# A hybrid decoder layer on one core: branch B's softmax exchange carried unit by unit and back in halves, with five smaller changes of order

## What is computed

```python
h = x @ w_in                                   # q, k, v, gate of both branches, two merge gates
# branch A: 16 heads of 64, 2 key/value heads, rope, causal window of 128, a sink logit per head
o_a = banded_attention(rope(qa), rope(ka), va, 127, sink=sinks)
# branch B: 4 heads of 128 in each of 3 groups, windows 128, 512, 2048 at dilations 1, 4, 16
for gi, (window, dilation) in enumerate(((128, 1), (512, 4), (2048, 16))):
    outs[gi], lses[gi] = dilated_group(rope(qb)[gi], rope(kb)[gi], vb[gi], window, dilation)
o_b = sum(softmax(lses, axis=0)[..., None] * outs)      # one softmax over the three groups
y_a = (o_a * silu(gate_a)) @ w_pa
y_b = (o_b * silu(gate_b)) @ w_pb
merged = sigmoid(mg_a + b0) * y_a + sigmoid(mg_b + b1) * y_b
out = layer_norm(1.189 * x + merged @ w_out, ln_g, ln_b)
```

## Time and profile before

| What | Value |
|---|---|
| Runs (three) | 1388.90, 1389.39, 1390.16 us, median 1389.39 |
| The profiled execution, device time | 1388.75 us |
| Span of its instructions | 1387.0 us |
| PE busy (matmuls) | 1360.5 us, 98% |
| PE busy in the last stretch, 1330 to 1387 | 43.6 of 57 us |
| ACT, POOL, DVE busy | 574.5, 669.8, 477.4 us (41, 48, 34%) |
| Granted TensorE clock, mean | 0.997 of full speed |

### The profile page before, as it was taken

How to read it: one execution, slowest core, us unless ns; L and a number is a source line. 1 busy time by engine, 2 the same in 40 slices (tenths; PEclk the granted TensorE clock), 3 DMA queues, 4 the chain that set the end, 5 groups by cost and what they waited for, 6 DMA issues and landing times.

```text
span 1387.0 us, 19876 instructions
## 1 busy us (share of the span) xinstructions
PE 1360.5 (98%) x6488; PEld 1154.3 (83%) x6488; DVE 477.4 (34%) x846; ACT 574.5 (41%) x971; POOL 669.8 (48%) x512
## 2 busy tenths in 40 slices
PE   9999999999999999999999999999999999999996
PEld 7888888778988988898898888888888888888884
DVE  5866565652031223203111011010101202287688
ACT  5455464543472365347237322222222222445442
POOL 4633443454555545455454465464555636422214
PEclk9999999999999999999999999999999999999998
DMA  8432241435374354337434343653536446377664
GB/s 260 131 122 76 76 136 52 130 111 119 93 168 137 87 120 135 119 92 163 147 110 137 88 149 113 151 129 102 177 91 157 122 130 147 95 248 259 208 241 152
DMA packets 204990, 190.07 MB, mean 137 GB/s; under 512 B 16528, under 2 KB 178576, under 8 KB 204944
## 3 DMA queue, kind: packets, MB, share of 16 engines
q1 hardware_dynamic: 191344, 151.74, 37.1%
q0 software_dynamic: 13600, 37.75, 11.0%
HBM read 185.23 MB, written 41.94 MB: 164 GB/s over the span
## 4 chain that ended last, share of the span: by engine, by line
PE 50%; issue 25%; POOL 20%; DVE 2%; ACT 1%; DMA 1%; POOLq 0%; SPq 0%; DVEq 0%; ACTq 0%
PE acc L1493 45%; POOL w_lo L574 11%; POOL w_lo L573 9%; PE ps_scores L1493 2%; PE ps_out L1493 1%; PE ps_turn L1493 1%; PE ps_out L1582 0%; DMA raw<-xT 0%; DMA raw<-w_in 0%; DVE w_lo L1290 0%; POOL q_left L599 0%; POOL q_left L601 0%; DVE x_lo L981 0%; DVE z L1351 0%; ACT both_stats L655 0%
## 5 line engine op out<-in xcount | busy, mean ns | idle before, releaser
L573 POOL TENSOR_TENSOR w_lo<-raw,w_hi 128x512 fp32r<-128x512 f32 x241 | 319.3, 1325 | 700.8 <-ACT w_hi L627 577.3
L1493 PE MATMUL acc<-x_hi,w_hi 128*128 128x512 f32 x1216 | 478.2, 393 | 5.8 <-POOL w_lo L574 3.2
L1493 PE MATMUL acc<-x_hi,w_lo 128*128 128x512 f32 x1216 | 474.2, 390 | 0.0
L1493 PE MATMUL acc<-x_lo,w_hi 128*128 128x512 f32 x1216 | 474.1, 390 | 0.0
L627 ACT ACTIVATE w_hi<-raw 128x1024 fp32r<-128x1024 f32 x224 | 234.5, 1056 | 337.2 <-PE acc L1493 332.5
L574 POOL TENSOR_TENSOR w_lo<-raw,w_hi 128x512 fp32r<-128x512 f32 x241 | 332.4, 1379 | 0.0
L1493 PEld LDWEIGHTS acc<-x_hi,w_hi 128*128 128x128 f32 x1216 | 228.5, 188 | 51.2 <-POOL w_lo L574 3.9
L1493 PEld LDWEIGHTS acc<-x_hi,w_lo 128*128 128x128 f32 x1216 | 228.2, 188 | 48.3
L1493 PEld LDWEIGHTS acc<-x_lo,w_hi 128*128 128x128 f32 x1216 | 228.5, 188 | 44.1
L1216 DVE TENSOR_TENSOR part_a<-acc,part_a 128x512 f32<-128x512 f32 x16 | 11.1, 691 | 321.7 <-PE acc L1493 321.7
L1493 PE MATMUL acc<-w_hi,x_lo 128*128 128x384 f32 x256 | 85.6, 334 | 0.0
(11 more groups left out here) (265 smaller groups left out, 1621.3 us busy)
## 6 DMA issues: line engine op xcount, KB each, us to landing
raw<-w_in SPq DMA_DIRECT2D x384, 128.0 KB, 2.3
q_left<-w_out POOLq DMA_DIRECT2D x12, 2048.0 KB, 13.6
raw<-w_in SPq DMA_DIRECT2D x256, 96.0 KB, 2.5
raw<-q_left SPq DMA_DIRECT2D x32, 512.0 KB, 4.8
raw<-w_in SPq DMA_DIRECT2D x64, 192.0 KB, 2.9
raw<-w_pa SPq DMA_DIRECT2D x64, 128.0 KB, 6.2
raw<-w_out SPq DMA_DIRECT2D x16, 512.0 KB, 4.2
raw<-xT SPq DMA_DIRECT2D x8, 512.0 KB, 4.7
```

What stands on the lines that cost most here:

```text
L573: nc.gpsimd.tensor_tensor(dst[:, left], raw[:, slot, left], hi[:, left].bitcast(F32), ALU.subtract)
L1493: ins = nc.tensor.matmul(into[:, 0:cols], s, m, start=start and k == 0, stop=stop and k == n - 1)
```

## The change

The change has six parts. No work is added or left out; two line numbers that the text names for the changed kernel are its own.

1. **The first job.** The matmuls of job 0 are reordered: all four high-by-high ones first (they wait for `w_hi` and `x_hi` only), then four of `w_lo` by `x_hi` after the low part of the weights, then four of `w_hi` by `x_lo` after the first `x_lo`.
2. **Branch A's values.** The low part of the probabilities comes last (order hi-hi, v_lo by probsT_hi, v_hi by probsT_lo, each over both key blocks), and the wait for it (`probsT_rest`) is moved from before the first matmul to before the third kind. This touches 32 units.
3. **Ropes.** `rope` is split in a cosine and a sine part, and the bank is given back by the cosine product. In the first head's group 0, the cosine product of tile 2 is put ahead of tile 1's sine product and sum.
4. **The exchange.** `collect` is done unit by unit, 4 copies a unit, one unit at a time from block 3 on (in the merge from block 1 on); `spread` in two halves of 8 copies, at its block and one later, with the divisions of units 2 and 3 waiting for one half each. The numbers of both plans change.
5. **The last stage, who makes what.** The low part of job 53 goes from DVE to POOL and that of job 54 from POOL to DVE.
6. **The last stage, when.** `row_root(1)` on ACT moves from job 49 to job 50 in its list, `row_far(1, 3)` on DVE from job 51 to job 54.

The diff, cut to its core:

```diff
-def head_stages(scores, apart, collect, mix, weigh, factor, spread, division, turn, values, gate):
+def head_stages(scores, apart, collect, mix, weigh, factor, spread, division, turn, values, gate, together=1):
...
+    for u in range(B_UNITS):
+        plan.setdefault(collect + u * apart, []).append(("collect", u))
+    for name, start in (("mix", mix), ("weigh", weigh), ("factor", factor), ("spread", spread), ("gate", gate)):
         plan.setdefault(start, []).append((name, 0))
+    plan.setdefault(spread + together, []).append(("spread", 1))
...
-B_PLAN = head_stages(1, 2, 9, 11, 12, 13, 14, 17, 19, 21, 28)
-B_PLAN_MERGE = head_stages(0, 1, 4, 5, 5, 6, 6, 7, 8, 9, 13)
+B_PLAN = head_stages(1, 2, 3, 10, 11, 12, 14, 16, 18, 20, 28)
+B_PLAN_MERGE = head_stages(0, 1, 1, 5, 5, 6, 7, 7, 8, 9, 13)
...
-POOL_LOW = (0, 1, 16, 17, 18, 32, 33, 34, 35, 44, 46, 50, 52, 54)
+POOL_LOW = (0, 1, 16, 17, 18, 32, 33, 34, 35, 44, 46, 50, 52, 53)
...
-            def collect(i, first_unit):
+            def collect(b, i, first_unit):
-                act.wait_ge(probs_ready, first_unit + B_UNITS)
+                act.wait_ge(probs_ready, first_unit + b + 1)
                 act.wait_ge(mixed, i * MIX_STEPS)
                 for r in range(NR):
-                    for b in range(B_UNITS):
-                        last = nc.scalar.activation(both_stats[rows_of(b), :, 0, r], near_stats[rows_of(r), :, b], ACT.Copy)
+                    last = nc.scalar.activation(both_stats[rows_of(b), :, 0, r], near_stats[rows_of(r), :, b], ACT.Copy)
...
-            def spread(i):
+            def spread(part, i):
                 act.wait_ge(mixed, i * MIX_STEPS + MIX_STEPS)
                 for r in range(NR):
-                    for b in range(B_UNITS):
+                    for b in (2 * part, 2 * part + 1):
...
-                    act.wait_ge(near_spread, i + 1)
+                    act.wait_ge(near_spread, i * 2 + (u - 1))
...
-                    if q == 49:
+                    if q == 50:
                         row_root(1)
...
-                nc.vector.tensor_tensor(to_order(dst), from_order(src), from_order(cos[:]), ALU.mult).then_inc(rope_parts, 1)
-                nc.vector.tensor_tensor(swapped_src, swapped_src, sin[:], ALU.mult).then_inc(src_free, 1)
+                nc.vector.tensor_tensor(to_order(dst), from_order(src), from_order(cos[:]), ALU.mult).then_inc(src_free, 1)
+            def rope_sine(dst, swapped_src, src_free, filled, done, branch, sin):
+                nc.vector.tensor_tensor(swapped_src, swapped_src, sin[:], ALU.mult).then_inc(rope_parts, 1)
                 dve.wait_ge(rope_parts, done + 1)
                 dve.wait_ge(src_free, filled)
...
+                        ahead = first and done_group == 0
+                        if not (ahead and tile == 2):
+                            rope_b_cosine(h, done_group, tile)
+                        if ahead and tile == 1:
+                            rope_b_cosine(h, 0, 2)
+                        rope_b_sine(h, first, done_group, tile)
...
-                    if q == 51:
+                    if q == 54:
                         row_far(1, 3)
...
                         if kind == "a":
-                            pe.wait_ge(probsT_rest, a + 1)
...
-                            for kb in kbs:
-                                for n, (v, p) in enumerate(((v_hi_a, probsT_hi), (v_hi_a, probsT_lo), (v_lo_a, probsT_hi))):
+                            for n, (v, p) in enumerate(((v_hi_a, probsT_hi), (v_lo_a, probsT_hi), (v_hi_a, probsT_lo))):
+                                if n == 2:
+                                    pe.wait_ge(probsT_rest, a + 1)
+                                for kb in kbs:
...
-            for e in range(8):
+            tiles = (ps_scores[:, 0:SEQ], ps_out[:])
+            pe.wait_ge(hi_done, 2)
+            for k in range(2):
+                for t in range(2):
+                    nc.tensor.matmul(tiles[t], w_hi[:, 0, first[k][t]], x_hi[:, k, :], start=k == 0, stop=False)
+            pe.wait_ge(lo_done, 1)
...
+            pe.wait_ge(x_lo_done, 1)
...
+            for e in range(1, 8):
```

More of the change, by code:

```diff
@@ L121, in head_stages @@
             plan.setdefault(start + u * apart, []).append((name, u))
-    for name, start in (("collect", collect), ("mix", mix), ("weigh", weigh), ("factor", factor), ("spread", spread), ("gate", gate)):
+    for u in range(B_UNITS):
+        plan.setdefault(collect + u * apart, []).append(("collect", u))
+    for name, start in (("mix", mix), ("weigh", weigh), ("factor", factor), ("spread", spread), ("gate", gate)):
         plan.setdefault(start, []).append((name, 0))
+    plan.setdefault(spread + together, []).append(("spread", 1))
     return plan
-B_PLAN = head_stages(1, 2, 9, 11, 12, 13, 14, 17, 19, 21, 28)
-B_PLAN_MERGE = head_stages(0, 1, 4, 5, 5, 6, 6, 7, 8, 9, 13)
+B_PLAN = head_stages(1, 2, 3, 10, 11, 12, 14, 16, 18, 20, 28)
+B_PLAN_MERGE = head_stages(0, 1, 1, 5, 5, 6, 7, 7, 8, 9, 13)
 def groups(spec, together=2):
@@ L709, in attend @@
                     if stage == "collect":
-                        collect(i, first_unit)
+                        collect(u, i, first_unit)
                     if stage == "weigh":
@@ L713, in attend @@
                     if stage == "spread":
-                        spread(i)
+                        spread(u, i)
                     if stage == "division":
@@ L1007, in rope @@
                 nc.vector.tensor_tensor(to_order(dst), to_order(dst), from_order(swapped_src), ALU.add).then_inc(rope_done, 1)
+            def rope(dst, swapped_src, src, src_full, src_free, filled, done, branch, cos, sin):
+                rope_cosine(dst, src, src_full, src_free, filled, done, branch, cos)
+                rope_sine(dst, swapped_src, src_free, filled, done, branch, sin)
             def masked(dst, scores, mask, scale, least):
@@ L1187, in rope_q, with rope_b_cosine, rope_b_sine @@
                 rope(q_a[:, j, :], (shifted, shifted_a)[j][:], acc[j][:], full[j], free[j], fills_a(j, i) + 1, ropes_a(i, j), "a", cos_a, sin_a)
+            def rope_b_cosine(h, group, tile):
+                rope_cosine((q_b, k_b)[group][:, tile, :], acc[tile][:], full[tile], free[tile], fills_b(tile, h) + (group + 1),
+                            ropes_b(h, 3 * group + tile), "b" if tile else "a", cos_b)
+            def rope_b_sine(h, first, group, tile):
+                rope_sine((q_b, k_b)[group][:, tile, :], swap_place(first, group, tile), free[tile], fills_b(tile, h) + (group + 1),
+                          ropes_b(h, 3 * group + tile), "b" if tile else "a", sin_b)
             def iter_b(h, first):
@@ L1198, in iter_b @@
                             dve.wait_ge(scores_ready, unit_b(h))
-                        rope((q_b, k_b)[done_group][:, tile, :], swap_place(first, done_group, tile), acc[tile][:],
-                             full[tile], free[tile], fills_b(tile, h) + (done_group + 1), ropes_b(h, 3 * done_group + tile),
-                             "b" if tile else "a", cos_b, sin_b)
+                        ahead = first and done_group == 0
[4 more added lines that the diff above has]
+                        rope_b_sine(h, first, done_group, tile)
                     if last and group == 1 and bank == 3:
@@ L1589, in _ @@
                 nc.tensor.transpose(ps_turn[:, 0:P], ident[:], ident[:])
-            for e in range(8):
+            tiles = (ps_scores[:, 0:SEQ], ps_out[:])
+            first = [[slice(256 * k + P * t, 256 * k + P * t + P) for t in range(2)] for k in range(2)]
+            pe.wait_ge(hi_done, 2)
[3 more added lines that the diff above has]
+            pe.wait_ge(lo_done, 1)
+            for k in range(2):
+                for t in range(2):
+                    nc.tensor.matmul(tiles[t], w_lo[:, 0, first[k][t]], x_hi[:, k, :], start=False, stop=False)
+            pe.wait_ge(x_lo_done, 1)
+            for k in range(2):
+                for t in range(2):
+                    nc.tensor.matmul(tiles[t], w_hi[:, 0, first[k][t]], x_lo[:, k, :], start=False, stop=False)
+            started[0] = True
+            for e in range(1, 8):
                 m = e // 2
```

9 lines of the change are left out of this document (6 added, 3 removed).

## The result

The changed kernel takes 1380.67 us (median of six runs, 1378.47 to 1380.75); the kernel before, run beside it, 1389.73 (six runs, 1388.90 to 1390.16). The ratio is 0.9933, with a 95% interval from 0.9920 to 0.9946: faster, by 9.1 us. The forecast was 1379.9 and 9.5 us. The profiled execution took 1380.62 us with a span of 1378.8; before they were 1388.75 and 1387.0.

What follows compares the result with a forecast made beforehand. PE bounds the kernel, so only its gaps can give time: 0 + 0.94 + 2.93 + 3.66 + 0.2 + 1.76 = 9.49 us off 1388.75 gives 1379.26, plus 0.64 for the median 1379.9; 8 in 10 range 1377.8 to 1384.5.

Steps and rivals of the forecast that it cites:

- What bounds it: Whole program: PE issues without pause at the upper clock, so gains come only from places where PE stands still.
- The start, 0: First job: PE can start at 8.58 instead of 9.77, but waits 1.2 us at job 6; gain 0, at most 0.1.
- Values, 0.94: Branch A's values: two matmuls run during each of four waits, each gap shrinks by 0.235; 0.94 us in all.
- rival (b): Branch A's values: the added wait stops weight loads, 32 times 0.188 = 6.0 us lost, 1385.9; chance 0.08.
- (c): Branch A's values: the added wait lets PE run empty, 0.46 us for each of 32 units, 1394.6; chance 0.03.
- Ropes, 2.93: First B head: PE's waits for banks 1 and 2, 1.04 and 1.89, both go; 2.93 us, lower bound 2.0.
- Heads, 3.66: Heads 1 to 3: PE's wait for POOL's half of `w_lo` goes in each, 3 × 1.22 = 3.66 us; lower bound 1.0.
- rival (a): Heads' gap stays or returns in part, ACT late by other work; gain 5.8, 1383.6; chance 0.20, whole or in part.
- The feared waits at the heads' values: Heads 1 to 3: values stand earlier in the plan, so up to three new waits of 0.3 us are possible.
- Merge, 0.2: Merge: the 0.72 wait for division 0 goes, a new one of some 0.5 replaces it; bounds 0 and 0.72.
- The end, 1.76: Last stage: PE 3.0 earlier at the last job, DVE then bounds the last sum; gain 1.76, bounds 0.5 and 3.0.
- rival (d): Parts don't do what they say: 1378.7 if the start keeps 1.2, 1382.3 if ropes or end give half; no separate chance.

Runs made afterwards that it cites:

- part 3 alone: Only the ropes edit (cosine and sine split, bank given back by the cosine product) on the kernel before: 1386.16 against 1389.36 us, ratio 0.9976.

## Why the prediction was right

- **What bounds it.** Right: the gain of 8.1 us in the profiled execution is PE's gaps and nothing else; PE's busy time is 1360.5 before and 1359.5 after, from the same 6488 matmuls.
- **The start, 0.** Right. The gain was 1.2 to 2.3 us at 8.5, more than the 1.2 that I saw, and gone at 30, at `x_lo`. It went earlier than I said, at job 2 and after (14.71 and 20.89), not at job 6. What is left of it is smaller than the spread from execution to execution.
- **Values, 0.94.** Right in mechanism, short in size: 1.25 alone, and 1.56 in that stretch of the full change, where 0.3 comes from part 3. The term was mis-sized because I took off two matmuls and kept the rest of each gap. Three of the four waits all but vanished, and their restart with them, part of the 0.16 that I had myself put on every bracket. The 28 added waits cost nothing, and the gap of units 1 to 7 that would have shown rival (b) or (c) isn't there. My strict reading of the Trainium skill ("TensorE: Matmul & The Clock Gate", "Step-by-step: what each phase is for") that I priced there at 6.0 us, no weight load pulled past a wait, doesn't hold for a wait that has been met: the 28 units run on at 0.12 us a matmul.
- **Ropes, 2.93.** Right: 3.1 both times for the two waits of the first B head. That the same edit gains another 0.3 in branch A was missing from the sum.
- **Heads, 3.66.** Two of three right, head 1 wrong: +0.28 instead of −1.22. The step that failed is the one sentence on the load, "Its raw weights allow that just so: the last piece, issued at 388.0, lands 10.7 us later, at 398.7". That was one landing of one execution, beside a 2 MB transfer, and I treated it as fixed, with 0.7 us of margin before the copy. It isn't, and the change moves it: the eight copies of `collect` that I put "in time in which ACT was idle" were not all free. Four of them delay an earlier `high`, and with it transfer and load, by 0.87 us; the load landed 0.7 to 2.8 us later against PE than with the old exchange, 1.4 too late at worst and just in time at best. It is rival (a) in part; its "other work" of ACT did the harm by way of the load. The feared waits at the heads' values didn't come: there is none at `ps_out` L1607 in the heads.
- **Merge, 0.2.** Right to 0.1: the wait of 0.72 went and one of 0.34 took its place, where the forecast had 0.5.
- **The end, 1.76.** 1.30 in the full change, 1.87 alone; the mechanism (DVE's chain, last sum no longer waiting for PE) was right, and the run with `row_far` in two showed it by moving the bound back to PE. From the start of job 55's high part to the last sum the chain takes 13.13 us (1355.18 to 1368.31), where I had 13.44, and the load that starts it was 0.79 late against PE: 1.76 + 0.31 − 0.79 = 1.28. The same sum with that load's lateness gives the other three executions with this end to 0.02. The last job started at 1357.55, where I had 1363.6 less 7.7, 1355.9: 0.9 because PE came 6.8 early and not 7.7, 0.8 from the load. So the size varies with the landing of job 55's load: PE's gap before job 55 was between 0.25 and 1.05 us in the six executions that had `row_far` behind it or split.
- **Range.** 1380.67 lies inside 1377.8 to 1384.5 and 0.8 from the forecast. That the total is so near is partly luck: head 1 and the end were 2.0 too high, values and ropes 0.8 too low. They did not cancel in the profile; the medians were kinder, 9.06 of 9.49. In rival (d) the 7.1 us need ropes and end both to give half; either alone leaves 8.0 or 8.6.

## What to carry to other kernels

Where PE is busy 98% of the time, list its gaps one by one, count each from start to start, and ask of each not only who is late but who is late next: the exchange's wait was held first by ACT and right behind it by a load. Before moving small work into an engine's idle time, look at what stands behind it in that engine's order: here four copies of 0.21 us each put off the release of a slot, and so a load, by 0.87. A load that lands beside a large transfer of another queue has no fixed time; the margins of 0.5 to 0.7 us here were none, and moving the transfer by a few jobs cost nothing (no gain alone, 1.6 us in head 1 with the exchange). Before moving an operation later, look up which bank or buffer it gives back.

## What the runs showed of the hardware

- A standstill of PE of 1.94 us, at 1344.6 to 1346.6, was followed by 3.4 us at the lower clock level (granted clock 0.62 over the window from 1346.5 to 1351, then 1.00). So was the idle time of 2.33 us before 9.93 with part 3 alone (granted clock 0.50 from 11.4 to 14.8). One of 1.83 us before job 55 in the kernel before, at the earlier trace rows's 1366.55, was not: its matmuls behind it were 0.23 us apart. Nor was the longer one with `row_far` back at its old place, 2.05 us by the same count as the 1.94 and the 1.83 (start to start, less 0.2265), before 1356.05, with a granted clock of 1.00 from 1354 to 1364. So the length alone doesn't decide; what does was not tried.
- The last piece of the load that stands behind a 2 MB transfer landed 12.4 to 14.8 us after the issue of its first piece began, in each of three heads of the nine executions that have them side by side (for example 382.3 to 397.1 in the changed kernel, head 1). Over the whole program before, the median from issue to landing is 2.3 us for pieces of 128 KB.
- Loads differ from one execution to the next. PE's position at 30 us, which hangs on the loads of the start, varies by 1.1 us over thirteen profiled executions, and one more is 1.59 late by the lower clock. By 60 us up to 0.5 more is added. From 80 us to the end of branch A's iterations, executions of the same code agree to 0.15 us.
